# Another order of projection passes, other block lengths and a level sum in three additions, in a hybrid decoder layer

## The reference

```python
h = rms_norm(x, norm_pre_mix)                          # x: 1 x 2048 x 1024, float32
proj = h @ w_in                                        # 1024 -> 3400 columns
q, k, v, qi, ki, wi, hq, hf, hi, hg = split_columns(proj)
att_out = dsa_attention(rope(q), rope(k), v, rope(qi), rope(ki), wi)   # top 256 keys per query
f = lb + (1 - lb) * sigmoid(hf)                        # recurrence: 4 heads, state 128 x 128
S_t = diag(f_t) S_{t-1} + (1 - f_t) hi_t^T
hg_out = rms_norm(silu(hq_t) S_t) * silu(hg)
x = x + rms_norm(concat(att_out, hg_out) @ w_out)
x = x + rms_norm((silu(h2 @ w_gate) * (h2 @ w_up)) @ w_down)   # h2 = rms_norm(x)
```

## Time and profile before

| | |
|---|---|
| median of 3 runs | 3585.67 us (3583.17 to 3588.73) |
| the profiled execution | 3587.84 us, span 3586.0 us |
| granted clock of TensorE, whole span | 0.945 |
| busy: TensorE, VectorE, ScalarE, GpSimd | 92%, 65%, 42%, 7% |
| first stage | 0 to 959.7 us, then TensorE is idle to 971.8 us |
| products / recurrence blocks in it | 160 / 16 |

### The profile page before, as it was taken

The page is one execution under the profiler, slowest core; times in us unless marked ns, Lnnn a source line. Parts: engine busy times, 40 slices in busy tenths (PEclk is TensorE's granted clock), DMA queues, the critical chain, the costliest instruction groups (busy, mean ns, idle before and its releaser), DMA issues. The chain is left out here.

```text
span 3586.0 us, 46159 instructions
## 1 busy us (share of the span) xinstructions
PE 3310.8 (92%) x17984; PEld 2904.4 (81%) x17984; DVE 2319.4 (65%) x3705; ACT 1509.9 (42%) x2429; POOL 239.9 (7%) x413
## 2 busy tenths in 40 slices
PE   8999999988767799999879999998899999989998
PEld 8999999888656688888667888887788888868886
DVE  3466776777576666666777677777867765453445
ACT  3443544444354444343453444444544443333222
POOL 0000000000111100000110101010200000010000
PEclk9999999999856899999889999998999999989999
DMA  5424343322201312222422222123211212342233
GB/s 177 158 100 153 115 143 123 112 106 109 74 22 50 115 63 81 76 86 74 152 77 70 76 65 77 64 87 123 88 63 56 72 61 68 104 147 97 91 103 109
DMA packets 139626, 339.41 MB, mean 95 GB/s; under 512 B 14352, under 2 KB 35216, under 8 KB 132240
## 3 DMA queue, kind: packets, MB, share of 16 engines
q1 hardware_dynamic: 137104, 332.26, 27.1%
q10 hardware_dynamic: 2304, 4.20, 0.3%
HBM read 283.38 MB, written 53.02 MB: 94 GB/s over the span
## 5 line engine op out<-in xcount | busy, mean ns | idle before, releaser
L1868 PE MATMUL PJ_d<-h_hi,wd_hi 128*128 128x512 f32 x1408 | 560.2, 398 | 12.5 <-DVE h_lo L1658 12.4
L1870 PE MATMUL PJ_d<-h_hi,wd_lo 128*128 128x512 f32 x1408 | 552.0, 392 | 0.0
L1869 PE MATMUL PJ_d<-h_lo,wd_hi 128*128 128x512 f32 x1408 | 551.3, 392 | 0.0
L1412 ACT ACTIVATE wd_hi<-wd_raw 128x512 fp32r<-128x512 f32 x592 | 359.5, 627 | 276.0 <-DMA wd_raw<-in_w_gu 169.6
L1653 DVE TENSOR_TENSOR wd_lo<-wd_raw,wd_hi 128x512 fp32r<-128x512 f32 x592 | 395.8, 689 | 52.7 <-ACT wd_hi L1412 50.3
L697 PE MATMUL PJ<-w_hi,h_hi 128*128 128x342 f32 (+1 forms) x1280 | 417.6, 326 | 4.2 <-DVE w_lo L530 4.2
L698 PE MATMUL PJ<-w_lo,h_hi 128*128 128x342 f32 (+1 forms) x1280 | 410.5, 321 | 0.0
L699 PE MATMUL PJ<-w_hi,h_lo 128*128 128x342 f32 (+1 forms) x1280 | 410.3, 321 | 0.0
L1637 DVE CUSTOM_DVE_ANT_0 prob<-SA,bias 128x1024 f32<-128x1024 f32 (+7 forms) x192 | 170.3, 912 | 364.0 <-PE SA L1795 363.4
L1407 ACT ACTIVATE pT<-SA 128x512 f32<-128x512 f32 (+3 forms) x320 | 156.7, 532 | 568.0 <-PE SA L1821 568.0
L1833 PEld LDWEIGHTS SC<-V,pT 128*128 128x128 f32 x2176 | 292.5, 206 | 49.3 <-ACT pT L1407 37.9
(11 more groups left out here) (186 smaller groups left out, 5881.4 us busy)
## 6 DMA issues: line engine op xcount, KB each, us to landing
wd_raw<-in_w_gu SPq DMA_DIRECT2D x352, 256.0 KB, 2.9
wd_raw<-in_w_down SPq DMA_DIRECT2D x176, 256.0 KB, 2.6
w_raw<-in_w_in SPq DMA_DIRECT2D x20, 1368.0 KB, 6.1
w_raw<-in_w_in SPq DMA_DIRECT2D x20, 1352.0 KB, 6.1
row_h<-proj_d SPq DMA_DIRECT2D x16, 1024.0 KB, 8.4
wd_raw<-in_w_out SPq DMA_DIRECT2D x64, 256.0 KB, 3.7
proj_d<-stage SPq DMA_DIRECT2D x40, 342.0 KB, 5.4
proj_d<-stage SPq DMA_DIRECT2D x40, 338.0 KB, 3.6
```

The lines of the kernel that those rows point to most:

```text
L1412: s_.activation(w_hi[:, u % RING, :], w_raw[:, u % RING, :], ACT.Copy).then_inc(w_hi_ready, 1)
L1868: t.matmul(to, w_hi[:, r, w], h_hi[:, c, :], start=(c == 0), stop=False)
L1869: t.matmul(to, w_hi[:, r, w], h_lo[:, c, :], start=False, stop=False)
L1870: last = t.matmul(to, w_lo[:, r, w], h_hi[:, c, :], start=False, stop=(c == KD - 1))
```

## The change

It has three parts. The list of passes is another: superblock 1's attention columns go last, and superblock 2's right behind its own recurrence columns. New tiles are then turned behind products 36 to 39, 60 to 63, 100 to 103 and 140 to 143, and the recurrence columns of superblocks 0 to 3 are done at product 24, 64, 88 and 128 (before: 24, 64, 104 and 128). The blocks begin at products 29, 39, 49, 59, 69, 77, 85, 93, 102, 110, 118, 126, 135, 141, 147 and 153. And VectorE's one reduction over eight levels becomes three additions, of four, two and one levels of 128 elements, the first two in place and each waited for by the next.

```diff
-    PASSES = [(0, HG_COLS), (0, AT_COLS), (1, HG_COLS), (1, AT_COLS), (2, HG_COLS), (3, HG_COLS),
-              (3, AT_COLS), (2, AT_COLS)]
+    PASSES = [(0, HG_COLS), (0, AT_COLS), (1, HG_COLS), (2, HG_COLS), (2, AT_COLS), (3, HG_COLS),
+              (3, AT_COLS), (1, AT_COLS)]
...
-    begin = [29 + 43 * b // 4 for b in range(4)] + [72 + 10 * b for b in range(4)] + [112 + 6 * b for b in range(9)]
+    begin = [29 + 10 * b for b in range(4)] + [69 + 33 * b // 4 for b in range(8)] + [135 + 25 * b // 4 for b in range(5)]
...
-                v.tensor_reduce(asum[:, h % 2, :], am[:, h % 2].rearrange("p m t -> p t m"), AX_X, ALU.add)\
-                 .then_inc(am_ready, 1)
+                lv = am[:, h % 2]
+                link(v.tensor_tensor(lv[:, 0:4], lv[:, 0:4], lv[:, 4:8], ALU.add))
+                link(v.tensor_tensor(lv[:, 0:2], lv[:, 0:2], lv[:, 2:4], ALU.add))
+                v.tensor_tensor(asum[:, h % 2, :], lv[:, 0], lv[:, 1], ALU.add).then_inc(am_ready, 1)
```

## The result

The changed kernel takes 3620.27 us (median; 3619.13 to 3620.79), the one before 3585.4 us (3583.17 to 3588.73, now of four executions): ratio 1.0096, 95% interval 1.0079 to 1.0114. It is 34.9 us slower. The forecast was 3606 us, slower by 20, with a range that ended at 3616: the sign and most of the places were right, the size was too small by 15 us, and the time lies outside the range.

A forecast was written before the change was run, and what follows sets the result against it. TensorE, busy 92% of the span, was taken to bound the kernel. Terms 25.3 + 9.1 - 9.8 - 5 + 0.5 = +20 on the profiled 3587.84 us gave 3608, as median 3606 us; range 3586 to 3616.

The forecast's parts named there:

- Term 1: Block openings: TensorE waits where a split stands before ScalarE's squares or no product covers; 44.4 us against 19.1 before, +25.3.
- Term 2: Block 4's row load lands late for ScalarE's gates; TensorE pauses 7.3 us in block 3, plus 1.8 for clock: +9.1.
- Term 3: Second change of superblock moves to block 3's middle slots; block 4 loses 7.3 us, block 7 4.0: -9.8 us.
- kind (b): Pause at a block's end, where a weight chunk is split in the last slot but one; TensorE waits 5.32 us.
- Term 4: Block ends and level waits: the sum takes 1.46 us for 1.98, and empty-slot waits go; -5 us, range 0 to -8.
- the empty fourth slot: Waits of half a microsecond at the empty fourth slot go in blocks with eight products: -2.3 us.
- Term 5: Block 15's row load, issued at product 148 behind the constants, with gates one product sooner: +0.5 us, bound +3.
- The clock step: After a TensorE pause of 3.36 us or more the clock is half, costing 1.8 us; after 1.62 us it stays full.

The follow-up runs named there:

- b1: Changed kernel with a weight split standing last in a block done behind the next block's first decays (ScalarE) and first operands (VectorE): 3598.81 us, ratio 1.0039 to before.
- b2: Changed kernel with products of blocks of 6, 7 and 8 spread so one stands between opening and first decays: 3592.89 us, ratio 1.0018 to before.
- a4: Changed kernel with SyncE's load of block 4's rows put ahead of the weight load at product 64: 3608.23 us, ratio 1.0058 to before.
- a2: Kernel before with the new list of passes alone, block lengths and reduction as before: 3583.97 us, ratio 0.9990 to before.
- a3: Changed kernel with the one reduction put back in place of the three additions: 3620.98 us, ratio 1.0092 to before.
- b3: Changed kernel with weight splits in slot 7 done behind the logarithm on ScalarE and the new state on VectorE: 3596.98 us, ratio 1.0032 to before.
- a1: Kernel before with the three additions alone: 3586.96 us, ratio 0.9992 to before.
- c1: Changed kernel with a4's load, a slot table covering openings, held splits of b1 and b3, and fg_lo behind slot 7's turned tile: 3558.01 us, ratio 0.9919 to before.
- c5: As c1, but splits last in a block not held, and slot 7's splits and fg_lo moved from block 7 on only: 3552.92 us, ratio 0.9905 to before.

## Why the prediction was right in its places and short in its size

**Term 1, openings** (44.4 us forecast). The pauses of 3.9 us came in blocks 4, 5, 6 and 15 at 3.89, 3.89, 3.86 and 3.86, and their blocks cost 5.7, 6.4, 5.4 and 6.6 us against the 5.7 put on each. Right for these four, shown by b1 and b2; block 13's part failed, see below. Blocks 9 and 10 opened with 0.4 us of pause at half clock, as in block 9 of before.

**Term 2, the row** (9.1 us). 9.0, shown by a4. This was the step with the longest chain of rows, and the mechanism held. That the number did so well is partly luck: the issue came after 6.7 us for the 6.3 forecast, the landing took 7.8 for 8.4, and the two nearly cancel.

**Term 3, turned tiles** (-9.8). a2 tests the part for the second change of superblock, 7.3 less 1.5 of lateness in block 3: it gives -4.8 for -5.8. Block 4 gains 7.3, and blocks 2, 3 and 7 give back 0.5, 1.9 and 0.6. The other 4.0, block 7's, no run tests alone; in the new order its turned tiles stand at block 7's end and at the opening of block 8, where I counted 3.0 and the pause is 1.21.

**Block 13, the step that failed.** Term 1 charged its opening (7.0), and the 0.4 us of its other waits stayed, 7.4 in all; it has 13.3 us of excess. The opening's pauses came as forecast, 1.22 and 2.98 us, with half clock behind them. The waits behind the opening were put at nothing more than before, and that failed: with the block beginning at 141 in place of 142, three turned tiles (products 141 to 143) and not two lie in its first five slots, and the split behind product 144 in the sixth. TensorE waits for the split of a turned tile before decays 2, falls to half clock once more, and waits twice at the end:

```profile
868.77 0.50 PE L730 MATMUL SA_p<-sums,fg_hi 128*128 128x512 f32 x1 [1.83 <-DVE h_lo L524]
...
890.00 1.80 PE L741 MATMUL SA_p<-qe,ke 128*128 128x128 f32 x14 [1.03 <-issue]
893.83 1.13 PE L763 MATMUL SA_p<-row_h,khat 128*128 128x128 f32 x8 [1.59 <-DVE am L588]
```

That is 4.4 us of pauses, and a second stretch at half clock, where I had put 0.4. I had walked through VectorE's queue for block 3 but not for block 13. The two runs that differ in the block lengths alone have 4.5 (a2) and 13.9 us (a3) there, so the lengths are the cause; no run puts block 13's beginning back alone, so which of them it is is read from the trace and not shown.

**Block 2, overlooked.** Product 56 is divisible by four and lies in slot 7 of the new block 2, a place of kind (b) that my list left out. Its slot 8 holds two products and covers most of it: 1.06 us of pause, 1.8 of excess. b3 holds that split back, and the pause is gone.

**Term 4, ends** (-5). The pauses were 4.93, 4.9 and 4.9 us, as forecast, and b3 shows that the chain with the split in it sets them. Block 7's was 6.0, where block 12 of before had 5.5. The additions give 2 us (a1, a3) for the 2.7 put on them; the 2.3 put on the empty fourth slot no run tests. The summed instructions are 692, 425 and 293 ns, 1.41 us for 1978 ns, as worked out from the rows. The Trainium skill (VectorE: DVE Perf Modes, "The perf-mode tier table") sets tensor_reduce and an fp32 tensor_tensor at one tier; by their times here, 1978 and 1218 ns at 1024 elements, one tier was not one speed.

**Term 5, the row of block 15** (+0.5). In block 14 ScalarE waits 3.02 us for that row, TensorE 1.5 us before the key-value matmuls, and the block has 4.1 us of excess for the 2.1 that terms 1 and 5 put on it.

In sum the forecast put 20 us on the first stage, and it is 28.8: 5.9 more in block 13, 2.0 in 14, 1.8 in 2, 0.9 in 15 and 0.7 ahead of block 1; the other blocks came out 2.5 cheaper together.

**What the range left out.** The second stage has no edit, and I held its length fixed. From its first matmul to the end it takes 2614.2 us before, 2616.7 after, and between 2609.4 (b1) and 2616.9 (a4) in the profiled executions of the other kernels, with no relation to the length of the first stage. The 2.5 us are within that spread. The 3.6 us between the profiled executions and the medians I could not know either, but a spread of 3 us on both sides was visible in the runs shown. A range that ended at +28 us on a sum of five terms, each read from single rows, had no room for an overlooked place: its upper end should have had one more pause with its clock, about 8 us by the costliest ones here (6.03 and 1.8). Without block 13's 5.9 us the time would have lain just inside the range.

The clock step held as well, for the pauses it was used on. In the first stages of all fourteen traces, from 205 us on, each of the 64 pauses of 3.5 us or more stands beside a stretch at half clock (1.2 for 2.4 GHz), and none of the 43 of about 1.62 us does. The Trainium skill (TensorE: Matmul & The Clock Gate, "Why this matters for your kernels") warns of idle gaps between bursts of matmuls; for the long pauses the traces agree. In between it goes both ways: a pause of 3.44 us in a3 left the clock full, and that of 1.83 us in block 13 was followed by half clock. So the clock's part is no constant: over the four openings the block's excess less the pause is 1.6 to 2.7 us, where 1.8 was put on each from one row.

## What to carry to other kernels

When work is interleaved by a fixed order, count what stands just ahead of each synchronising step on every engine, for every block, before asking how evenly the work is spread: one conversion of 2.5 us ahead of the squares cost 5.4 to 6.6 us in each of four blocks, and holding others back was worth 5.2 to 6.5 each. List all blocks mechanically; the ones I did in my head by analogy (2 and 13) are those that were wrong. And before a step is held back, look at what the DMA queue has in order behind it: a weight load that waits also holds the load of the next tile and the stores of the products.

## What was not expected of the hardware

One load held back holds everything that SyncE has in order behind it, and in c1 the cost is about the hold. SyncE issued c1's weight load of product 140 at 15.0 us after block 13's opening, for 6.2 in c5: 8.8 us later. ScalarE then sat idle 9.39 us for the x load, TensorE 9.00 us, and the block took 9.1 us more than c5's.

The savings of separate pauses add up here, and more: a4, b2 and b3 save 11.0, 23.5 and 20.8 us of first stage, 55.3 together. c1, which combines them with further moves, saves 59.3, and c5, which leaves out some of the held splits, 67.1. Which of the further moves gives the excess over 55.3 was not taken apart.
